# Hybrid attention layer on one NeuronCore: low parts of the output weights and sums of squares placed on other engines

## The chip, the cores and the metric

The kernel runs on one core of one Trainium2 chip. The metric is the time of one execution on the device, in microseconds (us). Lower is better. The five engines of a core are named as the profile names them: PE (TensorE, matmuls), PEld (its weight loads), DVE (VectorE), ACT (ScalarE), POOL (GpSimd) and SP (SyncE, which here only issues DMAs).

## The reference

One decoder layer over 256 tokens of width 1024, all in float32:

```python
h = rms_norm(x, norm_pre_g)                      # x * rsqrt(mean(x*x) + 1e-6) * g
proj = einsum('bsd,de->bse', h, w_in)
q_a, k_a, v_a, g_a, f_a, q_b, k_b, v_b, g_b = split(proj)
log_f = log_sigmoid(f_a + fox_forget_b)          # 8 heads
y_a = fox_attention(q_a, k_a, v_a, log_f) * silu(g_a)    # logits + F[t] - F[s], F = cumsum(log_f)
y_b = moba_attention(q_b, k_b, v_b, slopes) * silu(g_b)  # one block of 256: causal, ALiBi
y = einsum('bse,ed->bsd', concat(y_a, y_b), w_out)
out = x + rms_norm(y, norm_post_g)
```

Two groups of 8 heads of 64 columns. The sequence is one block of the second group, so both groups are dense causal attention over 256 positions.

## The kernel before

**Precision.** A float32 operand is split in a high part (rounded to the type that PE multiplies) and a low part (what is left over), and a product is three matmuls: high by high, high by low, low by high (`PASSES`). For weights, ACT copies the raw tile into the high part (`unit_high`, L354; for the output weights `out_unit_high`, L358), and then a subtraction gives the low part: on DVE for the input weights (`unit_low`, L538), on POOL for the first four tiles of the output weights (`out_unit_low`, L313).

**Weights.** The input weights come in 32 units of 128x1024 float32 (512 KB): units 0 to 7 for the values, 8 to 15 for the gates, 16 to 31 for queries and keys in turn. They pass through a ring of four slots: SP loads `raw`, ACT writes `w_hi`, DVE writes `w_lo`, PE multiplies. SP may load a slot again when its low part is done (`s_lo`), ACT may write the high part again when PE has used the unit (`s_used`). The first four tiles of the output weights have tiles of their own, `wo_hi` and `wo_lo`, and come through two slots `raw_out`; SP waits for the low part of tile 0 before it loads tile 2 (`s_olo`, L215), and so on. The other four follow the last units through the ring.

**Stages.** Every engine has one instruction stream, written out by hand; semaphores couple them, and a wait holds up all that stands behind it on its engine.

1. Values (until 35 us). x comes transposed (`x_t`). ACT and DVE make `xg_hi` and `xg_lo` (x times the gain of the norm), PE multiplies units 0 to 7 (L791), between them the eight columns of the forget gate (L805). The sums of squares of x: ACT squares `x_t` in four pieces (L367), POOL adds the pieces (L279, L280), and PE sums over the partitions with a vector of ones (L826), after unit 3. From that sum DVE and ACT make the mean square, its root (L389) and `rstd` (L564 to L571), DVE makes two diagonal matrices (L575), and after unit 5 PE spreads `rstd` over all partitions (L834). DVE copies it to `rrow` (L587).
2. Decay. DVE makes the logits of the forget gate (L592 to L596), ACT applies exponential and logarithm (L403, L405), DVE takes the running sum (L604). The rows go to DRAM and come back spread over all partitions, 1 MB, into `decay`, a name for the tile `squares` (L415, L425). POOL adds the mask to them: `fox_bias` (L285).
3. Gates (35 to 62 us), two rounds of four units: `gate_round` on DVE and on ACT. PE multiplies a unit (L775); DVE makes the low part of a unit ahead and multiplies the gate product by `rrow` (L612), which frees the PSUM bank: PE may start unit u only when the product of unit u-2 is taken over. In the first round DVE also makes `h32`, the normed x, two slices per unit (L616); in the second it makes `h_lo` from it (L622), in two halves. ACT makes high parts of units, of output weights on odd steps, and `h_hi` (L419).
4. Then ACT applies SiLU to all gates at once (L469), which waits for the last gate product, and the attention begins: per pair of heads a query and a key unit, scores, row maxima, exponentials, their sums' inverses, normalization by POOL (L302), transposes, values. The first query product waits for `h_lo`.
5. The output product (L932) and the last norm, until 161 us.

POOL runs in this order: constants, the sums of squares, `out_unit_low` 0 to 2, `fox_bias(0)`, `out_unit_low(3)`, then the attention's loops.

The lines of ACT that the steps speak of:

```python
nc.scalar.activation(fz[:, 1, :], fz[:, 1, :], ACT.Exp, scale=-1.0).then_inc(s_fexp, 1)     # L403
nc.scalar.activation(fz[:, 2, :], fz[:, 1, :], ACT.Ln, bias=1.0).then_inc(s_fln, 1)          # L405
unit_high(1, 48, 6)
```

Of the kernel before, what the change touches and what calls it, by code (L numbers as in the profile page):

```python
# [20 lines left out]
F32 = mybir.dt.float32  # L21
# [4 lines left out]
P = 128  # L26
# [27 lines left out]
def hybrid_layer(nc, xt, x, g_pre, w_units, w_f, f_bias, w_out, g_post, out):  # L54
# [8 lines left out]
    with ctx:  # L63
# [35 lines left out]
        rrow = sb("rrow", [P, SEQ])  # L99
        ms = sb("ms", [P, TT])  # L100
# [17 lines left out]
        y_post = h32[:, :, :].rearrange("p a b -> p (a b)").rearrange("p (t d) -> p t d", t=TT)  # L118
# [5 lines left out]
        ssq_ps, rrow_ps, f_ps = bank[6], bank[1], bank[7]  # L124
# [31 lines left out]
        s_sq, s_sqsum, s_ssq = sem("squares_done"), sem("square_sums"), sem("ssq_ready")  # L156
# [30 lines left out]
        def _(sp):  # L187
# [3 lines left out]
            for c in range(X_LOADS):  # L191
# [4 lines left out]
                if c == 0:  # L196
                    sp.dma_start(raw[:, c, HALF:], w_units[c, :, HALF:]).then_inc(s_raw_in[c], 16)
                else:
                    sp.dma_start(raw[:, c, :], w_units[c]).then_inc(s_raw_in[c], 16)
            sp.dma_start(fb_col[:, :], f_bias).then_inc(s_fb_in, 16)  # L200
# [43 lines left out]
        def _(pool):  # L244
# [31 lines left out]
            n = KT // X_LOADS  # L276
            for c in range(1, X_LOADS):
                pool.wait_ge(s_sq, c + 1)
                link(pool.tensor_tensor(squares[:, 0:n, :], squares[:, 0:n, :], squares[:, n * c:n * c + n, :], ALU.add))  # L279
            pool.tensor_tensor(squares[:, 0, :], squares[:, 0, :], squares[:, 1, :], ALU.add).then_inc(s_sqsum, 1)  # L280

# [29 lines left out]
            def out_unit_low(j):  # L311
                pool.wait_ge(s_ohi, j + 1)
                pool.tensor_tensor(wo[1][:, j, :], raw_out[:, j % 2, :], wo[0][:, j, :].bitcast(F32),  # L313
                                   ALU.subtract).then_inc(s_olo, 1)

            for j in range(OUT_OWN - 1):
                out_unit_low(j)
# [3 lines left out]
            out_unit_low(OUT_OWN - 1)  # L321
# [27 lines left out]
        def _(act):  # L349
# [12 lines left out]
            nc.scalar.activation(root[:, 0:1], ones[:, 0:1], ACT.Copy).then_inc(s_table, 1)  # L362
# [3 lines left out]
            def square(c):  # L366
                nc.scalar.activation(squares[:, n * c:n * c + n, :], x_t[:, n * c:n * c + n, :],  # L367
                                     ACT.Square).then_inc(s_sq, 1)

            for c in range(X_LOADS):  # L370
# [9 lines left out]
                else:  # L380
                    unit_high(c, 16)
                    square(c - 1)
            square(X_LOADS - 1)
            unit_high(0, 32, 1)
            unit_high(1, 32, 2)
            unit_high(2, 32, 3)
# [624 lines left out]
```

## Time and profile before

| | |
|---|---|
| median of 3 runs | 163.12 us |
| lowest, highest | 162.90, 168.15 us |
| span of the profiled execution (first to last instruction) | 161.2 us |
| what lies around the span, by the lowest run and by the median | 1.7, 1.9 us |
| busy, share of the span | PE 91%, PEld 80%, DVE 77%, ACT 70%, POOL 45% |
| granted clock of PE | 0.996 of full speed |

The time of the profiled execution itself is not given apart from its span; the runs stand 1.7 to 1.9 us above the span. A timeline row reads: start, duration, engine, line, operation, output and inputs, count; in brackets how long the engine was idle before it and what ended the idle time. Consecutive instructions of one line can be merged in one row, with their number at the end. A busy duration includes the time in which an instruction, once started, is held up.

### The profile page before, as it was taken

To read this page: it belongs to the slowest core of one execution; us is meant where nothing else is said; L and a number is where in the kernel's file an instruction comes from. 1 tells how busy PE (TensorE), PEld (TensorE's weight loads), DVE (VectorE), ACT (ScalarE), POOL (GpSimd) and SP (SyncE) were. 2 spreads that over 40 slices of the span, in tenths; PEclk is the share of its full clock that TensorE was granted. 3 is DMA by queue.
4 is the path that set the end of the run, shared out by engine and by line. 5 is a ranking of instruction groups with operands and counts; after the bars stand their busy time and mean duration, and the time that the engine had idled before them with its cause. 6 is when DMAs were issued, how large, how long until landed. Compare 5 with 4: busy or idle time off the path is not lost.

```text
span 161.2 us, 2896 instructions
## 1 busy us (share of the span) xinstructions
PE 146.4 (91%) x976; PEld 129.1 (80%) x976; DVE 124.8 (77%) x257; ACT 112.3 (70%) x228; POOL 72.0 (45%) x74
## 2 busy tenths in 40 slices
PE   7699999999958999999798999999998989999950
PEld 7267678889948999988687999998988867889850
DVE  0479976589999989685998989898989989340583
ACT  3589549398835874989959898979969696305330
POOL 7205910000960999504608475744719083501130
PEclk9999999999999999999999999999999999999998
DMA  3999376646796895591556455552526090000024
GB/s 56 304 413 355 123 247 217 250 130 242 262 372 205 357 296 193 169 256 69 150 179 185 140 172 159 139 189 64 157 108 195 0 319 10 0 0 0 4 85 175
DMA packets 12044, 27.99 MB, mean 174 GB/s; under 512 B 1272, under 2 KB 5376, under 8 KB 11776
## 3 DMA queue, kind: packets, MB, share of 16 engines
q1 hardware_dynamic: 11728, 26.52, 49.5%
q10 hardware_dynamic: 304, 1.32, 2.3%
q8 instruction: 7, 0.11, 0.3%
q14 instruction: 5, 0.04, 0.1%
HBM read 24.68 MB, written 1.06 MB: 160 GB/s over the span
## 4 chain that ended last, share of the span: by engine, by line
PE 33%; issue 25%; DVE 16%; POOL 12%; ACT 7%; DMA 3%; SPq 1%; POOLq 1%; DVEq 0%; ACTq 0%
PE bank L791 11%; PE bank L932 10%; PE bank L775 5%; POOL probs L302 5%; DVE w_lo L538 4%; DVE h L616 4%; POOL bias L285 3%; DMA raw<-in_w_units 3%; POOL bias L294 2%; ACT w_hi L354 2%; PE bank L805 2%; DVE h_lo L622 1%; PE bank L885 1%; POOL xg_lo L308 1%; ACT gate L469 1%
## 5 line engine op out<-in xcount | busy, mean ns | idle before, releaser
L538 DVE TENSOR_TENSOR w_lo<-raw,w_hi 128x1024 fp32r<-128x1024 f32 x35 | 51.4, 1475 | 3.7 <-ACT w_hi L354 3.4
L354 ACT ACTIVATE w_hi<-raw 128x1024 fp32r<-128x1024 f32 x35 | 36.8, 1057 | 6.9 <-PE bank L775 2.1
L775 PE MATMUL bank<-h_hi,w_hi 128*128 128x256 f32 x128 | 35.9, 280 | 0.0
L775 PE MATMUL bank<-h_lo,w_hi 128*128 128x256 f32 x128 | 35.8, 279 | 0.0
L775 PE MATMUL bank<-h_hi,w_lo 128*128 128x256 f32 x128 | 35.7, 279 | 0.0
L302 POOL TENSOR_TENSOR probs<-probs,row_inv 128x256 f32<-128x256 f32 (+1 forms) x16 | 12.9, 829 | 36.4 <-DVE row_inv L654 36.4
L313 POOL TENSOR_TENSOR wo_lo<-raw_out,wo_hi 128x1024 fp32r<-128x1024 f32 x4 | 17.4, 4350 | 24.6 <-ACT wo_hi L358 24.6
L775 PEld LDWEIGHTS bank<-h_hi,w_hi 128*128 128x128 f32 x128 | 24.2, 189 | 0.5 <-DVE h_lo L622 0.2
L775 PEld LDWEIGHTS bank<-h_lo,w_hi 128*128 128x128 f32 x128 | 24.0, 188 | 0.2
L775 PEld LDWEIGHTS bank<-h_hi,w_lo 128*128 128x128 f32 x128 | 24.2, 189 | 0.0
L775 PE MATMUL bank<-xg_hi,w_hi 128*128 128x256 f32 x64 | 17.9, 280 | 2.5 <-DVE gate L612 2.5
L438 ACT ACTIVATE probs<-logits,neg_max 128x128 f32<-128x128 f32 (+1 forms) x32 | 14.2, 445 | 8.6 <-DVE neg_max L649 8.6
L775 PE MATMUL bank<-xg_lo,w_hi 128*128 128x256 f32 x64 | 17.8, 279 | 0.0
L775 PE MATMUL bank<-xg_hi,w_lo 128*128 128x256 f32 x64 | 17.8, 279 | 0.0
L775 PEld LDWEIGHTS bank<-xg_hi,w_hi 128*128 128x128 f32 x64 | 12.1, 190 | 2.7 <-DVE gate L612 2.7
L285 POOL TENSOR_TENSOR bias<-squares,causal 128x256 f32<-128x256 f32 (+1 forms) x8 | 13.0, 1644 | 0.0
L308 POOL TENSOR_TENSOR xg_lo<-y,xg_hi 128x256 f32 (+1 forms) x8 | 9.9, 1238 | 5.9 <-ACT xg_hi L444 5.9
L775 PEld LDWEIGHTS bank<-xg_lo,w_hi 128*128 128x128 f32 x64 | 12.0, 188 | 0.0
L775 PEld LDWEIGHTS bank<-xg_hi,w_lo 128*128 128x128 f32 x64 | 12.0, 188 | 0.0
L791 PE MATMUL bank<-w_hi,xg_hi 128*128 128x512 f32 x32 | 11.0, 426 | 0.1
L638 DVE TENSOR_TENSOR p_t_lo<-bank,p_t_hi 128x512 fp32r<-128x512 f32 (+1 forms) x16 | 8.2, 553 | 3.0 <-ACT p_t_hi L430 2.8
L791 PE MATMUL bank<-w_lo,xg_hi 128*128 128x512 f32 x32 | 10.1, 398 | 0.0
(127 smaller groups left out, 336.7 us busy)
## 6 DMA issues: line engine op xcount, KB each, us to landing
raw<-in_w_units SPq DMA_DIRECT2D x31, 512.0 KB, 4.1
raw_out<-in_w_out SPq DMA_DIRECT2D x4, 512.0 KB, 4.5
v_pair<-v SPq DMA_DIRECT2D x8, 256.0 KB, 4.3
raw<-in_w_out SPq DMA_DIRECT2D x4, 512.0 KB, 3.5
x_t<-in_xt SPq DMA_DIRECT2D x4, 256.0 KB, 5.5
squares<-decay_rows_scratch ACTq DMA_DIRECT2D x1, 1024.0 KB, 7.8
x_t<-in_x SPq DMA_DIRECT2D x1, 1024.0 KB, 5.2
out<-x_t SPq DMA_DIRECT2D x3, 256.0 KB, 2.1
```

What stands on the lines that cost most here:

```text
L285: last = pool.tensor_tensor(bias[:, :, lo:hi], decay[:, bass.ds(2 * i, 2), 0:hi - lo], causal[:, lo:hi].unsqueeze(1).to_broadcast((P, 2, h ...
L302: pool.tensor_tensor(probs[:, :, lo:hi], probs[:, :, lo:hi], row_inv[:, t::2].unsqueeze(2).to_broadcast((P, 2, hi - lo)), ALU.mult).then_i ...
L308: pool.tensor_tensor(y[1][:, bass.ds(i, 1), :], y32[:, :].unsqueeze(1), y[0][:, bass.ds(i, 1), :].bitcast(F32), ALU.subtract).then_inc(s_y ...
L313: pool.tensor_tensor(wo[1][:, j, :], raw_out[:, j % 2, :], wo[0][:, j, :].bitcast(F32), ALU.subtract).then_inc(s_olo, 1)
L354: nc.scalar.activation(w[0][:, s, :], raw[:, s, :], ACT.Copy).then_inc(s_hi, 1)
L438: nc.scalar.activation(probs[:, a, lo:hi], logits[:, a, lo:hi], ACT.Exp, bias=neg_max[:, c:c + 1], scale=SCALE, accum_out=row_sum[:, c:c + ...
L538: nc.vector.tensor_tensor(w[1][:, s, :], raw[:, s, :], w[0][:, s, :].bitcast(F32), ALU.subtract).then_inc(s_lo, 1)
L616: nc.vector.scalar_tensor_tensor(out=h32[:, j, :], in0=x_t[:, j, :], scalar=gpre_col[:, j:j + 1], in1=rrow[:, :], op0=ALU.mult, op1=ALU.mu ...
L638: nc.vector.tensor_tensor(dst[1][:, :, :], src, dst[0][:, :, :].bitcast(F32), ALU.subtract).then_inc(s_ptlo, 1)
L775: last = nc.tensor.matmul(dst, stationary(a, j), moving(b, j), start=n == 1, stop=n == count * len(PASSES))
L791: last = nc.tensor.matmul(v_banks[c][t][:, :], xg[a][:, j, t * P:(t + 1) * P], w[b][:, u % RING, n * HALF:(n + 1) * HALF], start=j == 0 an ...
L932: last = nc.tensor.matmul(dst, y[a][:, p, t * P:(t + 1) * P], wide, start=p == 0 and (a, b) == PASSES[0], stop=p == PAIRS - 1 and (a, b) = ...
```

## The change

The low parts of output tiles 0 to 3 move from POOL to DVE, each behind an odd step of the gate rounds. The sums of squares are made by ACT alone: x is loaded once more, in rows (1 MB, into the tile of `h32`, which is free until the gates), and two activations square a row block each and add up along the row (`accum_out`). POOL's additions and PE's four small matmuls go. The first activation is a square root, so that its table is loaded at the start; the table that has both exponential and logarithm is loaded by name behind the root. Unit 6 is handled later: its high part behind the root on ACT, its low part behind the diagonals on DVE. SP issues the extra load of x behind unit 3.

```diff
@@ sync
+            sp.dma_start(x_rows, x).then_inc(s_xrows_in, 16)
             sp.dma_start(fb_col[:, :], f_bias).then_inc(s_fb_in, 16)
@@ gpsimd
-            n = KT // X_LOADS
-            for c in range(1, X_LOADS):
-                pool.wait_ge(s_sq, c + 1)
-                link(pool.tensor_tensor(squares[:, 0:n, :], squares[:, 0:n, :], squares[:, n * c:n * c + n, :], ALU.add))
-            pool.tensor_tensor(squares[:, 0, :], squares[:, 0, :], squares[:, 1, :], ALU.add).then_inc(s_sqsum, 1)
...
-            for j in range(OUT_OWN - 1):
-                out_unit_low(j)
             pool.wait_ge(s_pool, done[0])
             pool.wait_ge(s_decay_in, 16)
             fox_bias(0)
-            out_unit_low(OUT_OWN - 1)
@@ scalar
-            nc.scalar.activation(root[:, 0:1], ones[:, 0:1], ACT.Copy).then_inc(s_table, 1)
+            nc.scalar.activation(root[:, 0:1], ones[:, 0:1], ACT.Sqrt).then_inc(s_table, 1)
...
-            def square(c):
-                nc.scalar.activation(squares[:, n * c:n * c + n, :], x_t[:, n * c:n * c + n, :],
-                                     ACT.Square).then_inc(s_sq, 1)
+            def row_squares(t):
+                nc.scalar.activation(junk[:, t, :], x_rows[:, t, :], ACT.Square,
+                                     accum_out=row_ssq[:, t:t + 1]).then_inc(s_ssq, 1)
...
-                    square(c - 1)
-            square(X_LOADS - 1)
+            act.wait_ge(s_xrows_in, 16)
+            row_squares(0)
             unit_high(0, 32, 1)
+            row_squares(1)
             unit_high(1, 32, 2)
-            unit_high(2, 32, 3)
             act.wait_ge(s_ms, 1)
             act.wait_ge(s_table, 1)
             nc.scalar.activation(root[:, :], ms[:, :], ACT.Sqrt).then_inc(s_root, 1)
+            unit_high(2, 32, 3)
+            act.preload_act_table_set("natural_log_exp_and_others")
@@ vector
-            for u in range(X_LOADS - 1, 7):
+            for u in range(X_LOADS - 1, 6):
                 unit_low(u % RING, u + 1)
-            dve.wait_ge(s_ssq, 1)
-            nc.vector.tensor_scalar(ms[:, :], ssq_ps[:, 0:TT], 1.0 / D_MODEL, EPS, ALU.mult, ALU.add).then_inc(s_ms, 1)
+            dve.wait_ge(s_ssq, TT)
+            nc.vector.tensor_scalar(ms[:, :], row_ssq[:, :], 1.0 / D_MODEL, EPS, ALU.mult, ALU.add).then_inc(s_ms, 1)
...
+            unit_low(2, 7)
             unit_low(3, 8)
...
+            def out_unit_low(j):
+                dve.wait_ge(s_ohi, j + 1)
+                nc.vector.tensor_tensor(wo[1][:, j, :], raw_out[:, j % 2, :], wo[0][:, j, :].bitcast(F32),
+                                        ALU.subtract).then_inc(s_olo, 1)
...
+                    if s % 2:
+                        out_unit_low(r * 2 - V_UNITS // 2 + s // 2)
@@ tensor
-            value_unit(3)
-            pe.wait_ge(s_sqsum, 1)
-            for t in range(TT):
-                last = nc.tensor.matmul(ssq_ps[:, t:t + 1], squares[:, 0, t * P:(t + 1) * P], ones[:, 0:1],
-                                        start=True, stop=True)
-            last.then_inc(s_ssq, 1)
-            for u in range(4, 6):
+            for u in range(3, 6):
                 value_unit(u)
```

What DVE's stream is in the first gate round, before: a low part of a unit (`w_lo`), the gate product, two slices of `h` (the tile of `h32`), and again.

```order
L538 TENSOR_TENSOR w_lo<-raw,w_hi 128x1024
L612 TENSOR_TENSOR gate<-bank,rrow 128x256
L616 SCALAR_TENSOR_TENSOR h<-x_t,gpre_col,rrow 128x256 x2
L538 TENSOR_TENSOR w_lo<-raw,w_hi 128x1024
L612 TENSOR_TENSOR gate<-bank,rrow 128x256
L616 SCALAR_TENSOR_TENSOR h<-x_t,gpre_col,rrow 128x256 x2
L538 TENSOR_TENSOR w_lo<-raw,w_hi 128x1024
L612 TENSOR_TENSOR gate<-bank,rrow 128x256
```

The same place now:

```order
L529 TENSOR_TENSOR w_lo<-raw,w_hi 128x1024
L609 TENSOR_TENSOR gate<-bank,rrow 128x256
L613 SCALAR_TENSOR_TENSOR h<-x_t,gpre_col,rrow 128x256 x2
L529 TENSOR_TENSOR w_lo<-raw,w_hi 128x1024
L609 TENSOR_TENSOR gate<-bank,rrow 128x256
L613 SCALAR_TENSOR_TENSOR h<-x_t,gpre_col,rrow 128x256 x2
L601 TENSOR_TENSOR wo_lo<-raw_out,wo_hi 128x1024
L529 TENSOR_TENSOR w_lo<-raw,w_hi 128x1024
```

Behind every second step stands one subtraction more (`wo_lo`), four over the two rounds; the fourth stands behind the last gate product.

ACT's stream around the root and the decay, before, from the high part of unit 3 on (`squares` are the pieces of x squared, `logits` those of the forget gate):

```order
L354 ACTIVATE w_hi<-raw 128x1024
L367 ACTIVATE squares<-x_t 128x512 x2
L354 ACTIVATE w_hi<-raw 128x1024 x3
L389 ACT_TABLE_LOAD
L389 ACTIVATE root<-ms 128x2
L354 ACTIVATE w_hi<-raw 128x1024
L395 ACTIVATE v<-bank,rstd 128x512 x2
L354 ACTIVATE w_hi<-raw 128x1024
L403 ACT_TABLE_LOAD
L403 ACTIVATE logits<-logits 8x256
L405 ACT_TABLE_LOAD
L405 ACTIVATE logits<-logits 8x256
```

The same place now:

```order
L343 ACTIVATE w_hi<-raw 128x1024
L356 ACTIVATE squares,row_ssq<-h 128x1024
L343 ACTIVATE w_hi<-raw 128x1024
L356 ACTIVATE squares,row_ssq<-h 128x1024
L343 ACTIVATE w_hi<-raw 128x1024
L378 ACTIVATE root<-ms 128x2
L343 ACTIVATE w_hi<-raw 128x1024
L380 ACT_TABLE_LOAD
L343 ACTIVATE w_hi<-raw 128x1024
L386 ACTIVATE v<-bank,rstd 128x512 x2
L343 ACTIVATE w_hi<-raw 128x1024
L394 ACTIVATE logits<-logits 8x256
```

Three table loads have become one, and none stands any more between the exponential and the logarithm (the row behind the last one shown is the logarithm).

## Rows read from the trace of the kernel before

**Rows 1.** Page, parts 1 and 2: busy time, and slices of the span.
```profile
PE 146.4 (91%) x976; PEld 129.1 (80%) x976; DVE 124.8 (77%) x257; ACT 112.3 (70%) x228; POOL 72.0 (45%) x74
```

**Rows 2.** Chain that ended last, 23 to 63 us: start, us, what.
```profile
23.62 0.34 PE bank L826 x4
...
42.51 4.88 DVE h L616 x2
...
62.51 1.92 ACT gate L469
```

**Rows 3.** Windows: us, busy PE, PEld, DVE, ACT, POOL (count), PEclk, DMA share, GB/s.
```profile
35.13:40.60 5.47, 5.47 (x48) 5.42 (x47) 5.34 (x9) 4.70 (x7) 0.33 (x1) 1.00 0.74 272
...
46.00:48.90 2.90, 0.43 (x4) 0.23 (x3) 2.90 (x4) 1.06 (x1) 1.12 (x1) 1.00 0.89 352
```

**Rows 4.** Timeline of DVE, 30 to 64 us.
```profile
30.05 0.42 DVE L587 COPY rrow<-bank 128x256 f32<-128x256 f32 x1 [3.03 <-PE bank L834]
...
35.23 1.23 DVE L538 TENSOR_TENSOR w_lo<-raw,w_hi 128x1024 fp32r<-128x1024 f32 x1 [0.38 <-ACT w_hi L354]
...
42.44 4.95 DVE L616 SCALAR_TENSOR_TENSOR h<-x_t,gpre_col,rrow 128x256 f32<-128x256 f32 x2
47.33 1.21 DVE L538 TENSOR_TENSOR w_lo<-raw,w_hi 128x1024 fp32r<-128x1024 f32 x1
48.46 0.41 DVE L612 TENSOR_TENSOR gate<-bank,rrow 128x256 f32<-128x256 f32 x1
48.80 0.86 DVE L616 SCALAR_TENSOR_TENSOR h<-x_t,gpre_col,rrow 128x256 f32<-128x256 f32 x2
49.58 1.21 DVE L538 TENSOR_TENSOR w_lo<-raw,w_hi 128x1024 fp32r<-128x1024 f32 x1
...
53.31 1.20 DVE L622 TENSOR_TENSOR h_lo<-h,h_hi 128x1024 fp32r<-128x1024 f32 x1
...
57.70 0.42 DVE L612 TENSOR_TENSOR gate<-bank,rrow 128x256 f32<-128x256 f32 x1 [0.59 <-PE bank L775]
58.05 2.42 DVE L622 TENSOR_TENSOR h_lo<-h,h_hi 128x1024 fp32r<-128x1024 f32 x1
60.38 1.75 DVE L538 TENSOR_TENSOR w_lo<-raw,w_hi 128x1024 fp32r<-128x1024 f32 x1
62.06 0.41 DVE L612 TENSOR_TENSOR gate<-bank,rrow 128x256 f32<-128x256 f32 x1
```

**Rows 5.** Timeline of POOL in small windows, so that single instructions stand apart.
```profile
44.56 2.57 POOL L313 TENSOR_TENSOR wo_lo<-raw_out,wo_hi 128x1024 fp32r<-128x1024 f32 x1
...
52.27 7.11 POOL L313 TENSOR_TENSOR wo_lo<-raw_out,wo_hi 128x1024 fp32r<-128x1024 f32 x1 [5.15 <-ACT wo_hi L358]
59.34 1.72 POOL L285 TENSOR_TENSOR bias<-squares,causal 128x256 f32<-128x256 f32 x1
...
61.01 2.28 POOL L285 TENSOR_TENSOR bias<-squares,causal 128x512 f32<-128x512 f32 x1
```

**Rows 6.** Timeline of ACT: table loads and the high part behind them.
```profile
32.53 1.28 ACT L405 ACT_TABLE_LOAD   x1
...
34.15 1.04 ACT L354 ACTIVATE w_hi<-raw 128x1024 fp32r<-128x1024 f32 x1
```

**Rows 7.** DMA issues, whole span: count, KB each, median us to landing.
```profile
squares<-decay_rows_scratch ACTq DMA_DIRECT2D x1, 1024.0 KB, 7.8
x_t<-in_x SPq DMA_DIRECT2D x1, 1024.0 KB, 5.2
```

**Rows 8.** Timelines of ACT and SP: decay's issue, wo_hi, first loads' last, raw_out.
```profile
41.45 0.36 ACTq L425 DMA_DIRECT2D squares<-decay_rows_scratch  x1
...
51.13 1.06 ACT L358 ACTIVATE wo_hi<-raw_out 128x1024 fp32r<-128x1024 f32 x1 [0.22 <-DMA raw_out<-in_w_out]
...
6.43 0.40 SPq L200 DMA_DIRECT2D fb_col<-in_f_bias  x1
...
44.63 0.33 SPq L216 DMA_DIRECT2D raw_out<-in_w_out  x1
```

More of the change, by code:

```diff
@@ L99, in hybrid_layer @@
         rrow = sb("rrow", [P, SEQ])
+        row_ssq = sb("row_ssq", [P, TT])
         ms = sb("ms", [P, TT])
@@ L117, in hybrid_layer @@
         junk = squares[:, :, :].rearrange("p a b -> p (a b)").rearrange("p (t d) -> p t d", t=TT)
-        y_post = h32[:, :, :].rearrange("p a b -> p (a b)").rearrange("p (t d) -> p t d", t=TT)
+        x_rows = h32[:, :, :].rearrange("p a b -> p (a b)").rearrange("p (t d) -> p t d", t=TT)
+        y_post = x_rows
         decay_dram = nc.dram_tensor("decay_rows_scratch", (HEADS, SEQ), F32, kind="Internal").ap()
@@ L123, in hybrid_layer @@
         v_banks = [[bank[2], bank[3]], [bank[4], bank[5]]]
-        ssq_ps, rrow_ps, f_ps = bank[6], bank[1], bank[7]
+        warm_ps, rrow_ps, f_ps = bank[6], bank[1], bank[7]
         s0_ps = bank[2][:, 0:2 * P].rearrange("p (a n) -> p a n", a=2)
@@ L155, in hybrid_layer @@
         s_wfg, s_f = sem("wfg_ready"), sem("f_ready")
-        s_sq, s_sqsum, s_ssq = sem("squares_done"), sem("square_sums"), sem("ssq_ready")
+        s_xrows_in, s_ssq = sem("x_rows_in"), sem("row_squares")
         s_ms, s_root, s_rstd = sem("mean_square"), sem("root_ready"), sem("rstd_ready")
@@ L309, in y_low @@
                                    y[0][:, bass.ds(i, 1), :].bitcast(F32), ALU.subtract).then_inc(s_ylo, 1)
[L311 to L314, printed above, removed]
-            for j in range(OUT_OWN - 1):
-                out_unit_low(j)
             pool.wait_ge(s_pool, done[0])
@@ L811, in _ @@
             for n in range(WARM_UP):
-                nc.tensor.matmul(ssq_ps[:, 0:P], ones[:, :], ones[:, :], start=True, stop=True)
+                nc.tensor.matmul(warm_ps[:, 0:P], ones[:, :], ones[:, :], start=True, stop=True)
             pe.wait_ge(s_wfg, 1)
```

## The prediction

> **What bounds the kernel now.** I read the page's busy shares first: PE 91%, DVE 77%, POOL 45% [rows 1]. POOL's share says little, since it waits most of the time, so the question is where a POOL instruction holds something up. That is read from the chain that ended last [rows 2]. Until about 35 us it lies on PE; then it goes over to DVE, and its dearest DVE piece there is the pair of `h` slices at L616 with 4.88 us, in the first gate round. The same pair takes 0.86 us at 48.80 [rows 4]. PE pays for it: in the window 46.0 to 48.9 it is busy 0.43 of 2.90 us [rows 3], because a gate product may start only when the one two units before is taken over by DVE (L612). The reader is to see next that POOL's `wo_lo` runs in just these microseconds [rows 5]: one of 2.57 us from 44.56 to 47.13, and the DVE pair ends at 47.39. Three more DVE instructions are stretched the same way: `h_lo` 2.42 us at 58.05 where it takes 1.20 at 53.31, and `w_lo` 1.75 at 60.38 against 1.21 [rows 4] are two of them; POOL runs `wo_lo` until 59.38 and `bias` after it [rows 5]. So DVE instructions with two inputs in SBUF and POOL instructions hold each other up one whole instruction at a time, while the gate product of 57.70, one of whose inputs is a PSUM bank, kept its 0.42 us beside a running `wo_lo`. After the last gate product the chain goes through SiLU (1.92 us, ACT, 62.51) into the attention. From there to the end the change leaves every stream as it is, apart from the low part of output tile 3, which POOL no longer makes at 63 us. So the measure of the whole change is how much earlier the last gate product (62.06 to 62.47) ends and, beside it, `h_lo` (60.47), for which PE's first query product waits.
>
> **The parts of the change.** All terms are for the end of that last gate product.
>
> PE's small matmuls for the sums of squares go: 0.34 us [rows 2]. PE is in an unbroken row of matmuls there, and `rrow` waits for it (DVE idle 3.03 us at 30.05 [rows 4]), so this passes through: -0.34.
>
> Table loads. A load takes 1.28 us [rows 6]. Of the three that go or move, two lie in waits of ACT. The one at 32.53 stands between exponential and logarithm, and the high part at 34.15 behind it ends at 35.19; DVE waited 0.38 us for that one [rows 4, 6]. With the load gone DVE's own work is later than ACT's, so of 1.28 us only the wait comes back: -0.38.
>
> POOL's hold on DVE goes: the pair at 42.44, 4.95 - 0.86 = 4.09; `h_lo`, 2.42 - 1.20 = 1.22; `w_lo`, 1.75 - 1.21 = 0.54; together -5.85 [rows 4]. Where a stall goes something else is late next. PE's own pace is 48 matmuls in 5.47 us, 24 to a unit, so 2.74 us a unit [rows 3]. Its gates start 0.34 earlier, at 35.0, and eight units end at 56.9. Nothing on PE comes before that, and the wait of DVE for PE at 57.70 (0.59 us [rows 4]) goes if DVE is later than PE there, as it is below: -0.59.
>
> DVE gets the low parts of the output tiles: shape and operands are those of `w_lo`, 1.21 us, 1.13 from start to start (47.33 to 48.46 [rows 4]). Three stand ahead of the last gate product: +3.39. The fourth stands behind it, with 1.13 us, beside SiLU's 1.92 [rows 2]: 0. In a first-round step DVE then has 1.13 + 0.34 + 0.78 = 2.25 us, with a low part 3.38, so 2.82 on average against PE's 2.74; in the second round 2.6 with either an `h_lo` half or an output tile. DVE and PE are nearly even, which is why no more comes out than this sum. Each such low part waits for ACT's `wo_hi`, and unit low parts, gate products and `h_lo` are queued behind it, PE behind them. The tight one is tile 2: its high part started at 51.13, behind a transfer issued at 44.63 [rows 8], and ended at 52.2; DVE comes to it at about 53.4 without, 55.1 with the hold below: 0.
>
> What POOL keeps: `bias` of the first pair, two instructions. They ran at 59.34 and 61.01 [rows 5]. Alone they take what they held DVE up: about 0.6 (from the end of `h_lo`, 60.46, to 61.06) and 1.15 (from 62.13 to 63.29). Now POOL is free and starts as soon as the decay rows are back: issued at 41.45, 7.8 us to landing [rows 7, 8], some 0.4 to 0.8 earlier now, so at about 48.7. That is in the middle of DVE's busiest stretch. Bounds: 0 if POOL gets its turn only behind the last gate product, 1.75 if DVE stands still for both. I take 1.75, since the two `bias` rows each got their turn behind one DVE instruction: +1.75.
>
> The Trainium skill ("SBUF — State Buffer", section "Who interferes with whom") says that such a pair of instructions locks a shared port for the whole instruction and that the order of issue decides who waits. By that rule `bias`, once issued, waits for at most the DVE instruction in progress, and the term is 1.75; the trace agrees for `bias`, but not for the `wo_lo` of 52.27, which took 7.11 us beside several DVE instructions of 1.2 [rows 5]. By that row the term would be 0.
>
> ACT: four squares of x go and two activations over 1024 columns come, each about a high part's 1.04 us [rows 6] and a reading of the sum, for which I have no row at hand: between nothing and a load's 1.28 us. They stand in the values stage, where PE has its units well ahead. `rstd` is wanted by PE behind unit 5, and DVE idles 3.03 us before what follows from it: 0, and up to +1 if they were late beyond that cover. The extra load of x is 1 MB; the same transfer took 5.2 us [rows 7]. It is issued behind the loads of units 0 to 3, so it can delay unit 4 on, by 2.6 to 5.2 us at the most. Unit 6's low part, made later (behind the diagonals, at about 25), is wanted by PE only behind the spread of `rstd`, which DVE's copy of 30.05 follows: 0.
>
> Sum: -0.34 - 0.38 - 5.85 - 0.59 + 3.39 + 1.75 = -2.02 us. For `h_lo` the sum has no wait for the last two low parts and gives about -1.5, but PE's scores behind it wait for ACT's chain from SiLU (ACT is the later by then), so the larger shift holds. On the profiled span this is 161.2 - 2.0 = 159.2, and with the 1.9 us by which the median lies above the span, 161.1. In percent, 1.2; a measurement of this kernel can tell about 2% (3.3 us) from no change.
>
> **The rivals.**
>
> A. POOL does not get its turn in the gates. For it: `wo_lo` at 52.27 waited for about 4.8 us beside back-to-back DVE work [rows 5]. Against it: `bias` at 59.34 and 61.01 did not, and the `wo_lo` of 44.56 neither. Then the +1.75 falls away: -3.8 on the last gate product, and with PE's own end of the gates (60.5 to 57.1, or -3.4) close by. Time 163.1 - 3.6 = 159.5.
>
> B. The new wait on DVE takes the place of POOL's hold, slower than before. Place: `wo_lo` of tile 2 in the second gate round waits for its `wo_hi`, and this for its transfer. SP issues that transfer while the 1 MB of the decay, ACT's issue, is in flight; the DMA share is 0.89 then [rows 3]. The Trainium skill ("DMA: Bandwidth & Descriptors", "Queues, rings and completion order") says that a DMA engine takes turns between the queues, so that SP's transfers would go at half pace beside ACT's; the trace's row has 1 MB in 7.8 us. It decides from the point where the tile lands later than about 54: each us beyond is a us on the chain. To be slower than before, it must land 2 us later still, near 56, 12 us after issue; the measured issue to high part is 6.5 us [rows 8]. At 58 the price is 4 us: 163.1 + 2 = 165.1. Against it: loads of SP now come earlier, not later, and the sum of bytes is unchanged.
>
> C. The gain doesn't reach the end. The attention's loops have their own pace, in which POOL and DVE hold each other up as well, and another phase of the two could give 1 to 2 us back. For it: chain pieces through POOL there. Against it: every wait there is on work that moves by the same amount. Time 162.6, within 0.6 of before.
>
> D. The sums of squares come too late, because the load of x in rows is slow. PE then waits behind unit 5. The root must come 3 us later than before to cost anything [rows 4]. The load takes the place in SP's stream of the issue at 6.43 [rows 8]; with 5.2 us [rows 7] and as much again for the transfers in flight it lands by 17, and with two squares and two high parts of about 1.1 us ACT is through by 22, where the sum came from PE at 24 before. Time 162 to 163; it is within C's chance.
>
> **How the numbers follow.** The forecast, with both `bias` instructions or most of one in DVE's way, 0.52 (own range 160.3 to 161.9); A 0.22; C with D 0.19; B 0.07. The predicted time is the forecast's, 161.1. The range goes from 159.2 (A with its full 3.8) to 162.7 (C); outside lie B and the tails of A, somewhat under 0.2. Faster by over 2% means under 159.9: most of A's chance and little of the forecast's, 0.21. Slower by over 2% means over 166.4: B at its worst and what I haven't thought of, 0.04. Within 2%: 0.75.
>
> **What would show it.** In the profile after: the pairs at the line of `h32` all at 0.86 us; four `wo_lo` on DVE at 1.2 us without a wait for ACT ahead (a wait over 0.5 us is B); the `bias` pair of POOL near 49 us, and one or two DVE instructions beside it 0.6 and 1.15 us longer (none stretched is A); no idle stretch of PE over 1 us between 35 and 57 us; the last gate product ending at 60.4 (58.7 in A); one table load ahead of the exponential and none behind it; DVE idle over 2 us before `rrow`. The prediction is wrong if the last gate product moves as said and the end doesn't (C), or if PE idles before the spread of `rstd` (D).

## The result: 159.6 us, 3.5 to 3.8 us less than before

The changed kernel takes 159.58 us in the median (158.50 to 161.14, 4 runs) where the kernel before takes 163.33 (162.90 to 168.15, 4 runs: the three behind the table of before and one of 163.54). One execution of each, 168.15 and 161.14 us, was slow; the ratio and the medians in the table of experiments leave such runs out, and without it the median before is 163.12. The ratio is 0.975, with a 95% interval of 0.970 to 0.980; two more sets of runs of the changed kernel gave 0.976 (0.972 to 0.980) and 0.978 (0.972 to 0.984). The profiled execution took 159.58 us with a span of 157.7 (before: 161.2), so 1.9 us lie around the span, as assumed, and the spans differ by 3.5 us. The forecast was 161.1; the measured time is that of rival A, 159.5.

The page of the changed kernel, busy time and slices:

```profile
PE 145.0 (92%) x972; PEld 128.0 (81%) x972; DVE 119.0 (75%) x261; ACT 109.8 (70%) x226; POOL 57.7 (37%) x66
```

DVE has four instructions more than in [rows 1] and is busy 5.8 us less: more than that went of the time in which an instruction had started and stood still.

Timeline of DVE after, to be laid beside [rows 4] (the lines are 3 to 9 lower, `wo_lo` is L601):

```profile
29.80 0.42 DVE L579 COPY rrow<-bank 128x256 f32<-128x256 f32 x1 [3.31 <-PE bank L826]
...
34.51 1.22 DVE L529 TENSOR_TENSOR w_lo<-raw,w_hi 128x1024 fp32r<-128x1024 f32 x1
...
41.72 0.86 DVE L613 SCALAR_TENSOR_TENSOR h<-x_t,gpre_col,rrow 128x256 f32<-128x256 f32 x2
42.51 1.21 DVE L601 TENSOR_TENSOR wo_lo<-raw_out,wo_hi 128x1024 fp32r<-128x1024 f32 x1
...
50.44 0.41 DVE L609 TENSOR_TENSOR gate<-bank,rrow 128x256 f32<-128x256 f32 x1
50.77 1.20 DVE L619 TENSOR_TENSOR h_lo<-h,h_hi 128x1024 fp32r<-128x1024 f32 x1
51.90 1.21 DVE L529 TENSOR_TENSOR w_lo<-raw,w_hi 128x1024 fp32r<-128x1024 f32 x1
...
55.97 1.20 DVE L619 TENSOR_TENSOR h_lo<-h,h_hi 128x1024 fp32r<-128x1024 f32 x1
57.11 1.21 DVE L529 TENSOR_TENSOR w_lo<-raw,w_hi 128x1024 fp32r<-128x1024 f32 x1
58.24 0.41 DVE L609 TENSOR_TENSOR gate<-bank,rrow 128x256 f32<-128x256 f32 x1
58.58 1.21 DVE L601 TENSOR_TENSOR wo_lo<-raw_out,wo_hi 128x1024 fp32r<-128x1024 f32 x1
```

The pair of slices is at 0.86 us, `wo_lo` at 1.21, and nothing at all is stretched: not `h_lo`, not the `w_lo` beside it. The `w_lo` at 34.51 has no wait in brackets any more (0.38 us before), which is the table load. The last gate product ends at 58.65, before at 62.47: 3.82 us earlier.

POOL after, the answer to [rows 5], with `bias` as its only work there:

```profile
49.05 13.73 POOL L282 TENSOR_TENSOR bias<-squares,causal 128x256 f32<-128x256 f32 x2 [44.19 <-DMA squares<-decay_rows_scratch]
```

The two `bias` instructions need about 1.75 us alone, by the estimate of the prediction, and take 13.73. They ended at 62.78, so by that estimate they began to run at about 61.0, when DVE's unbroken stream of instructions with two SBUF inputs was over (60.92). POOL paid for all of it and DVE for none, and nobody waits for `bias`: the logits, its first reader, start at 68.08.

The chain of the changed kernel, 55 to 66 us, beside [rows 2]:

```profile
56.04 1.14 DVE h_lo L619
57.19 0.04 issue
57.23 5.74 PE bank L774 x48
...
63.80 1.06 ACT w_hi L343
...
66.09 0.36 PE bank L857
```

Before, it went from the last gate product into SiLU. Now the second `h_lo` releases PE's first two attention units (57.23 to 62.97), and they are later than ACT, which has SiLU and the high part behind it done at 62.84. So 3.82 us on the gate product become 3.47 at the first scores (69.56 before, 66.09 now), and 3.5 at the end.

### The profile page after: what moved, and what is told of

The parts are those of the page before. It is cut to its first block, busy times and chain, and to the rows that moved or that the text cites. A ratio compares the mean times of both kernels' runs of the same rounds, so it can differ in the third digit from the quotient of the medians.

```text
span 157.7 us, 2881 instructions
## 1 busy us (share of the span) xinstructions
PE 145.0 (92%) x972; PEld 128.0 (81%) x972; DVE 119.0 (75%) x261; ACT 109.8 (70%) x226; POOL 57.7 (37%) x66
## 4 chain that ended last, share of the span: by engine, by line
PE 33%; issue 25%; DVE 21%; POOL 12%; ACT 3%; DMA 3%; POOLq 1%; SPq 1%; DVEq 0%
PE bank L790 12%; PE bank L924 11%; DVE w_lo L529 7%; POOL probs L299 5%; PE bank L774 4%; POOL bias L282 3%; PE bank L804 3%; DMA wf<-in_w_f 3%; POOL bias L291 2%; DVE wo_lo L601 2%; DVE h L613 2%; DVE v L574 2%; DVE gate L609 1%; DVE h_lo L619 1%; POOL xg_lo L305 1%
## 5 line engine op out<-in xcount | busy, mean ns | idle before, releaser
L529 DVE TENSOR_TENSOR w_lo<-raw,w_hi 128x1024 fp32r<-128x1024 f32 x35 | 47.6, 1361 | 7.1 <-ACT w_hi L343 6.8
L282 POOL TENSOR_TENSOR bias<-squares,causal 128x256 f32<-128x256 f32 (+1 forms) x8 | 22.8, 2864 | 44.2 <-DMA squares<-decay_rows_scratch 44.2
L877 PE MATMUL bank<-p_t_hi,v_pair 128*128 128x512 f32 (+1 forms) x32 | 9.4, 346 | 0.7 <-DVE p_t_lo L637 0.3
```

Source lines behind the costliest of these rows:

```text
L282: last = pool.tensor_tensor(bias[:, :, lo:hi], decay[:, bass.ds(2 * i, 2), 0:hi - lo], causal[:, lo:hi].unsqueeze(1).to_broadcast((P, 2, h ...
L529: nc.vector.tensor_tensor(w[1][:, s, :], raw[:, s, :], w[0][:, s, :].bitcast(F32), ALU.subtract).then_inc(s_lo, 1)
L877: last = nc.tensor.matmul(dst, v_pair[:, b, x * TT + t, :], (p_t0, p_t1)[t][z][:, :, :], start=n == 0, stop=n == len(order) - 1)
```

## The experiments

**How the runs are compared.** Single runs of one kernel differ by 1 to 2 us, and the profiles show where: in the opening, before PE's third group of forget matmuls at about 16 us (it starts at 15.98 in the changed kernel and at 17.92 in e3, and from there to `rrow` both take 13.82). I therefore give, beside the time, the start of DVE's copy to `rrow` (the end of the opening, for every kernel the same instruction) and what of the span lies behind it. That last figure is 127.7 to 127.9 in three profiles of the changed kernel. A timed comparison stands beside it where there is one.

| kernel | median, us (runs) | span | `rrow` at | span behind it |
|---|---|---|---|---|
| before | 163.12 (3) | 161.2 | 30.05 | 131.1 |
| changed | 159.58 (3) | 157.7 | 29.80 | 127.9 |
| e1, `wo_lo` back on POOL | 162.77 (3) | 160.6 | 29.82 | 130.8 |
| e2, before with `wo_lo` on DVE | 160.47 (4) | 159.5 | 31.25 | 128.3 |
| e3, two table loads | 160.04 (3) | 160.0 | 31.74 | 128.3 |
| e4, old sums of squares | 160.94 (4) | 158.6 | 30.83 | 127.8 |
| e5, two POOL instructions, step 1 | 164.39 (1) | 162.6 | 30.97 | 131.6 |
| e6, the same, step 3 | 162.95 (1) | 161.0 | 29.93 | 131.1 |
| e7, `h_lo` with a constant | 159.29 (1) | 157.4 | 29.59 | 127.8 |
| e7, `h_lo` with a scalar in SBUF | 161.75 (1) | 159.8 | 30.42 | 129.4 |
| e8 and e10, `bias` ahead of the normalization | 159.09 (3), 159.64 (5) | 157.3, 157.7 | 30.23, 30.57 | 127.1, 127.1 |
| e9 and e14, changed again | 159.48 (4), 159.66 (6) | 157.5, 157.7 | 29.71, 29.96 | 127.8, 127.7 |
| e11, scalar in SBUF and late `bias` | 160.18 (1) | 158.3 | 30.34 | 128.0 |
| e12, late `bias` | 160.15 (6) | 157.5 | 29.55 | 128.0 |
| e13, e5 with `h` without the gain | 161.40 (1) | 159.6 | 28.90 | 130.7 |
| e15, e5 with waits on `h` | 162.35 (1) | 160.5 | 30.70 | 129.8 |
| e16, `h_lo` without a wait, late `bias` | 159.53 (1) | 157.6 | 29.83 | 127.8 |
| e17, `h_lo` in slices without a wait, late `bias` | 161.03 (1) | 159.2 | 30.82 | 128.4 |

**The parts, one by one: e1 to e4.** In e1 the four low parts go back to POOL, the rest stays changed:

```diff
@@ gpsimd
...
+            for j in range(OUT_OWN - 1):
+                out_unit_low(j)
...
             fox_bias(0)
+            out_unit_low(OUT_OWN - 1)
@@ vector
...
-                    if s % 2:
-                        out_unit_low(r * 2 - V_UNITS // 2 + s // 2)
```

> The changed kernel with one part undone: the four low parts of the output weights are on POOL again, at their old places. Theory 1 (what the change gains is DVE's release from POOL's two-tile hold in the first gate round): the pair of h slices takes 4 to 5 us again somewhere in the gates, PE idles 2 to 3 us, and the time is before's less the small terms 0.34 and 0.38, so about 162.5, ratio to before 0.994 to 1.0. Theory 2 (the gain comes from the front: squares and table loads): the time stays near the changed kernel's 159.6, ratio 0.975 to 0.98.

Measured 162.77 us, and behind `rrow` 130.8. DVE's timeline of e1 shows the old picture:

```profile
41.73 5.13 DVE L616 SCALAR_TENSOR_TENSOR h<-x_t,gpre_col,rrow 128x256 f32<-128x256 f32 x2
```

The pair is back at 5.13 us, and the two smaller holds with it (`h_lo` 2.73, `w_lo` 1.75). Theory 1 holds. e2 is the mirror image: the same diff with the signs turned, on the kernel before.

> The kernel before with this part alone: the four low parts of the output weights on DVE, squares and table loads as before. Theory 1: most of the gain, 3.8 less 0.7 of small terms, so about 160.2, ratio 0.98, and POOL's first bias waits over 5 us for a turn beside an unbroken DVE stream. Theory 2: nothing or a loss, ratio 0.995 to 1.01, since DVE gets 4.5 us of work more.

Measured 160.47 us, behind `rrow` 128.3. POOL in e2:

```profile
49.44 15.24 POOL L285 TENSOR_TENSOR bias<-squares,causal 128x256 f32<-128x256 f32 x2 [27.93 <-DMA squares<-decay_rows_scratch]
```

So the move of the low parts is worth 131.1 - 128.3 = 2.9 us on the kernel before and 130.8 - 127.9 = 2.9 us on the changed one. e3 takes the named table load away:

```diff
-            act.preload_act_table_set("natural_log_exp_and_others")
```

> The changed kernel without the named table load: the exponential and the logarithm load their own tables again (1.28 us each), the first in ACT's wait, the second between the two. Theory 1 (only DVE's wait for the high part behind counts): DVE waits about 0.4 us again, the time is 159.6 plus 0.4, ratio to before 0.977 to 0.98. Theory 2: the whole load counts, plus 1.3 us, ratio 0.983.

DVE's timeline of e3 has the wait of before again:

```profile
36.91 1.23 DVE L528 TENSOR_TENSOR w_lo<-raw,w_hi 128x1024 fp32r<-128x1024 f32 x1 [0.38 <-ACT w_hi L343]
```

Behind `rrow` it costs 128.26 - 127.9 = 0.4 us, not the 1.28 of the load. The medians differ by 0.46 (ratio to before 0.980, interval 0.974 to 0.985), which contains both 0.4 and nothing. e4 makes the sums of squares the old way:

```diff
-            sp.dma_start(x_rows, x).then_inc(s_xrows_in, 16)
-            row_squares(0)
...
-            row_squares(1)
...
+                    square(c - 1)
...
+                link(pool.tensor_tensor(squares[:, 0:n, :], squares[:, 0:n, :], squares[:, n * c:n * c + n, :], ALU.add))
...
+                last = nc.tensor.matmul(warm_ps[:, t:t + 1], squares[:, 0, t * P:(t + 1) * P], ones[:, 0:1],
+                                        start=True, stop=True)
```

> The changed kernel with the sums of squares made as before (ACT's squares of the transposed x, POOL's additions, PE's four small matmuls), no extra load of x. Theory 1: only PE's 0.34 us comes back, 159.9, ratio to before 0.979; DVE's low parts in the values stage are stretched to 1.8 to 2.3 us beside POOL's additions, and that costs nothing there. Theory 2: POOL's hold in the values stage reaches PE, ratio 0.985 or more.

Behind `rrow` nothing changes (127.8). From PE's third group of forget matmuls to `rrow` it is 14.28 us in e4 (16.55 to 30.83) and 13.82 in the changed kernel (15.98 to 29.80): 0.46, somewhat over the 0.34 of the four matmuls. The median is 1.4 us higher than the changed kernel's; of the 0.9 us by which the profiled span is longer, 0.6 is the opening (16.55 against 15.98). DVE's low parts beside POOL's additions were stretched and cost nothing:

```profile
16.23 6.21 DVE L533 TENSOR_TENSOR w_lo<-raw,w_hi 128x1024 fp32r<-128x1024 f32 x3
```

Three take 6.21 us instead of about 3.5, and PE doesn't notice. The parts add up: 2.9 + 0.4 behind `rrow` and 0.4 to 0.5 ahead of it, less 0.2 by which the changed kernel's opening happened to be later, make the 3.5 us of the span.

**Does POOL ever get its turn? e5 and e6.** Two POOL instructions with two SBUF inputs, about 1.15 us each alone, are added to the changed kernel, behind the first gate product (e5, shown) or the third (e6, with 3 in the wait). The 1.15 us is an estimate, that of the larger `bias`, which has the same number of columns:

```diff
+            pool.wait_ge(s_gmul, 1)
+            for part in p_t0:
+                pool.tensor_tensor(part[:, :, :], dist[:, P:NB].unsqueeze(1).to_broadcast((P, 2, SEQ)),
+                                   causal[:, P:NB].unsqueeze(1).to_broadcast((P, 2, SEQ)), ALU.mult)
             pool.wait_ge(s_decay_in, 16)
             fox_bias(0)
```

> The changed kernel with two more POOL instructions (512 columns each, about 1.15 us alone, both inputs in SBUF, a product of constants into a tile not yet in use) behind the first gate product, where the old wo_lo arrived. Theory 1 (a POOL instruction gets no turn while DVE's stream has no gap, whatever DVE runs): both take over 15 us to get through and DVE is not stretched. Theory 2 (POOL gets its turn between a gate product, which reads a PSUM bank, and the slices of h, as at 42.1 us before): one slice of h is stretched to about 1.6 us and the next again, DVE loses about 2.3 us, and the first bias is ready early.

> The same two POOL instructions, but behind the third gate product, so that the first gap of its kind that they meet is the one ahead of the slices of h in the fourth step. Theory 1: no DVE instruction stretched, both wait until DVE is idle at about 61 us. Theory 2: a slice of h in the fourth step is stretched; DVE loses up to 2.3 us and the time rises by as much.

Theory 2 in both. POOL and then DVE in e5:

```profile
40.85 3.24 POOL L311 TENSOR_TENSOR p_t_hi<-dist,causal 128x512 fp32r<-128x512 f32 x1 [36.00 <-DVE gate L613]
44.06 1.47 POOL L311 TENSOR_TENSOR p_t_lo<-dist,causal 128x512 fp32r<-128x512 f32 x1
48.20 2.31 POOL L282 TENSOR_TENSOR bias<-squares,causal 128x256 f32<-128x256 f32 x2 [2.66 <-DMA squares<-decay_rows_scratch]
```

```profile
42.89 2.92 DVE L617 SCALAR_TENSOR_TENSOR h<-x_t,gpre_col,rrow 128x256 f32<-128x256 f32 x2
...
48.34 2.44 DVE L617 SCALAR_TENSOR_TENSOR h<-x_t,gpre_col,rrow 128x256 f32<-128x256 f32 x2
```

The added pair costs DVE 2.06 us, and here `bias`, which arrived at 48.20 while a gate product ran and slices of `h` were next, cost it 1.58: both together make 3.64 of the 3.7 us that e5 has more behind `rrow`. In e6 the pair cost 2.05, and `bias`, directly behind it on POOL, held up `h_lo` by 0.21 and the next `w_lo` by 1.10; together 3.2 us more behind `rrow`. POOL's two `bias` rows of e6, each by itself:

```profile
50.09 3.18 POOL L282 TENSOR_TENSOR bias<-squares,causal 128x256 f32<-128x256 f32 x1
...
53.24 2.27 POOL L282 TENSOR_TENSOR bias<-squares,causal 128x512 f32<-128x512 f32 x1
```

The first ended at 53.27; it let a `wo_lo` and a `w_lo` go first and got in behind the gate product of 52.61, with `h_lo` next. So the forecast's price for `bias` (1.75) was about right for a `bias` that gets its turn, and its mistake was that it would.

**What decides it: e7, e11, e13, e15 to e17.** A lone arrival is here a POOL instruction with none directly before it. The lone arrivals that got in inside DVE's unbroken stream had one thing in common: a `w_lo` ended, a gate product ran, and slices of `h` were next. The slices have a scalar read from SBUF, 256 columns, and no semaphore wait. Seven kernels move these features about. The two of e7 write `h_lo` in the form of `h`, one with the constant shown, one with `ones[:, 0:1]`, a column in SBUF, in its place:

```diff
-                        nc.vector.tensor_tensor(h[1][:, part, :], h32[:, part, :], h[0][:, part, :].bitcast(F32),
-                                                ALU.subtract).then_inc(s_hlo, 1)
+                        nc.vector.scalar_tensor_tensor(out=h[1][:, part, :], in0=h32[:, part, :], scalar=1.0,
+                                                       in1=h[0][:, part, :].bitcast(F32), op0=ALU.mult,
+                                                       op1=ALU.subtract).then_inc(s_hlo, 1)
```

> The changed kernel with the two h_lo halves written as scalar_tensor_tensor with a constant scalar 1.0 (same operands, same values). POOL's first bias arrives at about 49 us and meets the first of them behind the gate product at 50.4. Theory 1 (the scalar_tensor_tensor form behind a gate product is what lets POOL in; plain tensor_tensor keeps it out): h_lo is stretched by 0.6, the instruction behind by 1.15, bias is over by 53 us, time up by 1.8 to about 161.3. Theory 2 (the form does not matter, or only the scalar in SBUF does): bias waits until about 61 us, time 159.6.

> The same with the scalar read from a column of ones in SBUF, as the slices of h read theirs from the gain. Theory 1: as with the constant, bias gets in at 50.4, time 161.3. Theory 2a (only a scalar in SBUF opens the door): here bias gets in and h_lo is stretched, and with the constant it does not. Theory 2b (the form does not matter; the state of the second round keeps POOL out): bias waits until 61 us in both, time 159.6.

With the constant `bias` took 15.02 us. With the scalar in SBUF it took 2.51, but not for the reason under test: in that execution it arrived at 47.56, ahead of the last slices of `h`, whose pair was stretched to 2.36. The two POOL rows, first the constant's, then the other's:

```profile
47.54 15.02 POOL L282 TENSOR_TENSOR bias<-squares,causal 128x256 f32<-128x256 f32 x2 [42.67 <-DMA squares<-decay_rows_scratch]
```

```profile
47.56 2.51 POOL L282 TENSOR_TENSOR bias<-squares,causal 128x256 f32<-128x256 f32 x2 [42.70 <-DMA squares<-decay_rows_scratch]
```

The arrival is the same to 0.02 us; DVE was 0.8 us later in the second, so that `bias` still met a gate product with slices behind it. It cost 1.5 us. e11 therefore adds `pool.wait_ge(s_h32, KT)` ahead of `fox_bias(0)` to the second of these:

> The changed kernel with h_lo as scalar_tensor_tensor with its scalar read from a column of ones in SBUF, and with bias held back until all slices of h are made, so that it cannot meet them. Theory 1 (a DVE instruction with a scalar in SBUF, behind a gate product, opens the door): bias arrives at about 48 to 49, gets in ahead of the h_lo at 50.8, which is stretched to about 1.8, and the next DVE instruction by 1.15; last gate product 1.7 us later. Theory 2 (only the first round lets POOL in, whatever the form): bias takes 13 to 15 us, nothing on DVE is stretched.

`bias` took 14.47 us, DVE was not stretched: the form of the instruction with its scalar in SBUF does not by itself let POOL in. e13 is e5 with `scalar=1.0` in the slices of `h`; this leaves the gain of the first norm out of h.

> The kernel with the two added POOL instructions in the first gate round, and the slices of h made with the constant 1.0 in place of the gain (this leaves the gain of the first norm out of h). Theory 1 (the scalar in SBUF opens the door): the two wait until DVE is idle at about 61 us, the slices of h stay at 0.86 a pair, and the time is about 159.6 plus what three more POOL instructions behind 61 us cost (0 to 2), not 164.4. Theory 2 (the form does not matter): a pair of slices is stretched to 2.9 us as before, 164 us.

The pair, 0.74 us without a hold, was stretched to 2.86 all the same, so the scalar in SBUF is not needed either:

```profile
40.69 2.86 DVE L617 SCALAR_TENSOR_TENSOR h<-x_t,rrow 128x256 f32<-128x256 f32 x2
```

e15 puts a wait (long met) ahead of each slice in e5. e16 moves the wait of `h_lo` ahead of the unit's low part, so that `h_lo` itself has none, and e17 besides cuts that `h_lo` in four slices of 256 columns; both hold `bias` back as e11 does.

> The kernel with the two added POOL instructions in the first gate round, and a semaphore wait that has long been met in front of every slice of h. Theory W (a DVE instruction that carries a wait keeps POOL out behind a gate product, one without lets it in): no slice of h is stretched, the two POOL instructions wait until about 61 us, time 160 to 161.5. Theory S (the size decides: 256 columns let POOL in, 1024 don't) or any other: one pair of slices takes 2.9 us again, time about 164.

> The kernel with the late bias, and the wait of h_lo moved ahead of the unit's low part, so that h_lo itself, 1024 columns, stands behind the gate product without a wait. Theory W: bias gets in ahead of the first h_lo at about 50.5 and both are stretched, by 0.6 and 1.15; last gate product 1.7 us later. Theory S: bias waits 13 to 15 us, nothing is stretched.

> As e16, and h_lo made in four slices of 256 columns each, without waits. Theory W and theory S both let bias in here behind the gate product; with e16 it tells size from wait: in here and not in e16 is S, in in both is W, in in neither and it is something else of the slices of h (their inputs or what they share with the gate product). The slices cost 0.4 us more per half by themselves.

DVE's row of e15, and POOL's of e16 and e17:

```profile
42.62 2.92 DVE L618 SCALAR_TENSOR_TENSOR h<-x_t,gpre_col,rrow 128x256 f32<-128x256 f32 x2
```

```profile
48.45 14.35 POOL L282 TENSOR_TENSOR bias<-squares,causal 128x256 f32<-128x256 f32 x2 [43.59 <-DVE h L616]
```

```profile
50.10 14.10 POOL L282 TENSOR_TENSOR bias<-squares,causal 128x256 f32<-128x256 f32 x2 [45.25 <-DMA squares<-decay_rows_scratch]
```

With waits the slices still let POOL in; without a wait `h_lo` still keeps it out; in slices too (they cost 0.21 us more per half, 1.41 against 1.20, where 0.4 was expected). So for `h_lo` neither the form, nor the missing wait, nor the small size together with the missing wait lets POOL in. Form, size and missing wait all together were not tried for `h_lo`. e15 also has a case against the pattern itself: its `bias` arrived at 50.27, 0.07 us before slices of `h` were to start, and waited 15.46 us. What remains is a regularity of places within the gates. Of the lone arrivals there, those that met a gate product with slices of `h` next got in in every other case, and those whose first gate product had `h_lo` next did not. The `bias` of e6, directly behind another POOL instruction, did get in ahead of `h_lo`.

The values stage of the kernel before shows that even this is not general. POOL's additions for the sums of squares, 128x512 like the added pair, also met DVE's `w_lo`, with no gate products between:

```profile
13.33 1.82 POOL L279 TENSOR_TENSOR squares<-squares 128x512 f32<-128x512 f32 x1 [8.46 <-ACT squares L367]
...
15.66 1.29 POOL L279 TENSOR_TENSOR squares<-squares 128x512 f32<-128x512 f32 x1 [0.52 <-ACT squares L367]
...
15.74 2.29 DVE L538 TENSOR_TENSOR w_lo<-raw,w_hi 128x1024 fp32r<-128x1024 f32 x1
```

Both additions are lone arrivals. The first was over in 1.82 us, behind the one `w_lo` in progress, and the second in 1.29, ahead of a `w_lo`, which took 2.29 us for it. So neither the lone arrival nor the form of `w_lo` keeps POOL out by itself; what is different in the gates stays open. How a long wait ends can be read from two rows of `wo_lo`: at a wider gap in DVE's stream. The `wo_lo` of 52.27 [rows 5] ended at 59.38 and needs about 2.3 us, so it began at about 57.1, where DVE waited 0.59 us for PE [rows 4]; that of 50.73 in e1 ended at 58.84, so it began at about 56.6, where DVE waited 0.28 us.

**The late bias and the other order: e12, e9, e14, e8, e10.** e12 is the changed kernel with `pool.wait_ge(s_h32, KT)` alone.

> The changed kernel with one wait more: POOL's first bias is held back until all slices of h are made, and so always arrives in the stretch of plain tensor_tensor. If the changed kernel's runs of 161 and more are those in which bias came just before the last slices, this one loses them and its median is 0.3 to 1 us lower than the changed kernel's in this call; if they come from elsewhere (the clock in the opening), the two agree within 0.3%.

> The changed kernel unchanged, as the measure for the one with the late bias: 159.6 us within 1 us.

160.15 us (ratio 0.983, interval 0.976 to 0.989) against 159.66 (0.978, 0.972 to 0.984) for the changed kernel timed beside it: no gain to be seen, and executions above 161 us occur with the late `bias` too. Its two, 161.4 and 161.6, have a mean granted clock of 0.972 against 0.997 of the profiled one, which fits the later openings described below. e8 lets POOL make the next pair's bias ahead of the normalization:

```diff
+            fox_bias(1)
             norm_probs(0)
-            fox_bias(1)
             with pool.Fori(2, FOX_PAIRS) as i:
-                norm_probs(i - 1)
                 pool.wait_ge(s_logits, 4 * i)
                 fox_bias(i)
+                norm_probs(i - 1)
                 y_low(i - 2)
...
```

> The changed kernel, and in the attention POOL makes the bias of the next pair ahead of the normalization of the current one instead of behind it. Theory 1 (POOL's normalization, bias and xg_lo stand in series on the chain of each pair, 1.3 us of bias in it): up to 1.3 us less for each of 6 pairs, 5 to 7 us less than 159.6. Theory 2 (the attention is held by PE and DVE anyway, POOL's waits give way): 0 to 1.5 us less. A third: bias delays the normalization where DVE holds it up, and the time rises by 1 to 3 us.

> The changed kernel unchanged, as the measure for the others of this call: 159.6 us within 1 us, ratio to before 0.975.

> The changed kernel with POOL's bias ahead of its normalization, timed beside the changed kernel. If the attention is held by PE and DVE, the two agree within 0.3% (159.3 to 159.8); if the order is worth something, it is 0.5 to 1 us faster.

e8 came to 159.09 us, and the same kernel again (e10) to 159.64 beside 159.48 for the changed kernel (e9). Theory 1, 5 to 7 us, is refuted. Behind `rrow` both profiles have 127.1 against 127.7 to 127.9, so 0.7 us are there, but their `rrow` came 0.3 to 0.9 us later and the times overlap. It beats both kernels by that reading only; timed it is no different from the changed kernel.

## Why the prediction was wrong

The direction, the place and the rivals were right, the size was not: 161.1 forecast, 159.6 measured, and the change of 3.5 to 3.8 us is 1.7 to 1.9 times the 2.0 of the sum.

- **PE's small matmuls, -0.34.** 0.44 (from the third forget group to `rrow` 14.26 before, 13.82 now). Right.
- **Table loads, -0.38.** Right: the wait is gone, e3 brings 0.38 back on DVE and 0.4 behind `rrow`.
- **POOL's hold, -5.85 with -0.59 for DVE's wait.** Right: no instruction of the list is stretched and there is no wait for PE ahead of the seventh gate product. e1 brings all three holds back.
- **Three low parts on DVE, +3.39.** Right: 1.13 us from start to start each, no wait for `wo_hi` ahead of any. Rival B did not occur; tile 2's high part ended at 51.7, DVE came to it at 53.4.
- **`bias`, +1.75. This is the step that failed.** The value was taken "since the two `bias` rows each got their turn behind one DVE instruction". In those rows `bias` stood directly behind another POOL instruction, as in e6, where it cost DVE 1.31 us. Here it arrived alone, at 49.05, in an unbroken stream of DVE instructions, did not get in for 12 us and cost DVE nothing. The row of 52.27 [rows 5], to which the prediction gave less weight, was the nearer one: also a lone arrival whose first gate product had `h_lo` next. That the lone arrival makes the difference is not shown, and rows speak against it: in e5, e7 and e13 a lone `bias` got in ahead of slices of `h`, and the lone additions of the values stage got in behind one DVE instruction. So the term that failed is known and its mechanism is open. Without this term the sum is -3.77 for the last gate product; measured -3.82. That the two agree so closely says that the other terms were right together.
- **ACT's squares and the load of x in rows, 0.** Right, and inside the bounds given. The landing took 9.6 us from issue, where 5.2 and as much again was allowed; ACT waited 1.42 us for the rows and was through with both sums at 19.4, where 22 was allowed. The reading of a sum, for which the prediction had no row, takes 0.19 us, and DVE's copy to `rrow` still has 3.31 us of idle time ahead of it.
- **From the gate product to the end.** "So the larger shift holds" was not quite so: `h_lo` ends 3.30 us earlier (60.47 before, 57.17 now), PE's first units, released by it, are the later chain now, and 3.82 shrinks to 3.47.

The rule of the Trainium skill on the shared port ("SBUF — State Buffer", "Who interferes with whom") was followed in its second half, that the order of issue decides. Here the trace differs: `bias` was issued at 49.05 and let nine DVE instructions of 1.2 us that stand behind the one then in progress go first. The first half, the lock for a whole instruction, holds: each stretched DVE pair is longer by about POOL's whole instructions. Gate products, with one input in PSUM, kept 0.40 to 0.43 us everywhere.

## What to carry to other kernels

When an instruction's duration is far over that of its neighbours of the same shape, look at what the engine that shares its port was doing, and price the move of that work by shape and not by its busy time: three subtractions of 1.13 us on DVE ahead of the last gate product, and a fourth behind it, replaced holds of 5.85 us. Before assuming who wins when two engines meet, look for rows in the same stage with the same neighbours: here one row (52.27) foretold the case and several others did not, and what told them apart was found in no experiment; then the forecast should give both outcomes their weight. And when single runs scatter more than the effect, split the span at an instruction that all variants share.

## What the hardware showed unexpectedly

- A POOL instruction with SBUF inputs can be kept out for 12 to 14 us by back-to-back DVE instructions with two SBUF inputs, although every 2.6 us a gate product, with one input in PSUM, leaves about 0.3 us between them. The same POOL instruction got in within 0.3 us in e5 (0.87 us for the smaller `bias`, which takes about 0.6 alone). The long wait (13.7 to 15.5 us for the pair) stands in fourteen profiles of this study, its condition is not found, and in the values stage POOL's additions waited for one DVE instruction at most.
- The opening varies from run to run of one kernel. Windows of the changed kernel and then of e3, 8 to 13 us (columns as in [rows 3]):

```profile
8.00:11.00 3.00, 3.00 (x9) 2.00 (x9) 1.75 (x4) 2.28 (x5) 0.00 (x0) 1.00 1.03 412
11.00:13.00 2.00, 2.00 (x9) 1.30 (x8) 2.00 (x4) 1.90 (x5) 0.00 (x0) 1.00 1.07 435
```

```profile
8.00:11.00 3.00, 2.73 (x6) 1.83 (x6) 1.89 (x5) 2.27 (x5) 0.00 (x0) 0.50 1.02 399
11.00:13.00 2.00, 2.00 (x6) 0.45 (x5) 2.00 (x4) 1.85 (x4) 0.00 (x0) 0.50 1.09 442
```

In e3 PE was granted 0.50 of full speed there, so 1.2 GHz, after 1.12 us of idle time ahead of the first value matmul; the second group of four forget matmuls took 1.81 us on its chain instead of 0.96, and `rrow` came 1.9 us later. From 17 to 150 us the granted clock is 1.00 in both. Six more profiles (e7 with the scalar in SBUF, e8, e10, e11, e15, e17) have 0.50 to 0.62 from 8 to 11 us. The granted clock of the rows is not all of it: e5's is 1.00 throughout the opening, and still its second group of four forget matmuls took 1.67 us and `rrow` came at 30.97.
- The 1 MB load of x in rows took 9.6 us to landing behind the first loads, the 1 MB of the decay 5.9 to 8.3 us in the different profiles: one row is no bound for a transfer in traffic.
